# Where the square sums of each norm are made, and when attention bias and expert weights are asked for, in a hybrid SSD / RWKV-7 / attention / MoE trunk

## The reference

```
mod   = silu([c_ctx, c]) @ w_mod + b_mod               # 6 x 1024 values for context, 6 x 1024 for latent
h     = rmsnorm(x) * norm1 * (1 + mod[1]) + mod[0]     # adaLN, first norm
ssd   = rmsnorm(scan(h) * silu(z(h))) * ssd_norm       # branch A, with a norm of its own
rwkv  = ...                                            # branch B
att   = softmax(q k^T / 8 + na_bias + mask) v          # branch C, 2-D neighbourhood attention
x    += mod[2] * ((sum over branches of sigmoid(gate_b) * (branch_b @ w_branch_b)) @ w_out)
h     = rmsnorm(x) * norm2 * (1 + mod[4]) + mod[3]     # second norm
x    += mod[5] * moe(h)                                # 16 experts, two for each token
out   = rmsnorm(x_latent) * final_norm                 # after both layers
rmsnorm(x) = x / sqrt(mean(x * x) + 1e-6)
```

## Time and profile before

| what | us |
|---|---|
| median of 3 runs | 4776.42 |
| lowest and highest | 4769.83, 4780.67 |
| the profiled execution's own time | 4769.36 |
| its span, first to last instruction | 4767.6 |

### The profile page before, as it was taken

The page is one execution under the profiler, slowest core; times in us unless marked ns, Lnnn a source line. Parts: engine busy times, 40 slices in busy tenths (PEclk is TensorE's granted clock), DMA queues, the critical chain, the costliest instruction groups (busy, mean ns, idle before and its releaser), DMA issues. The chain is left out here.

```text
span 4767.6 us, 98189 instructions
## 1 busy us (share of the span) xinstructions
PE 4123.0 (86%) x42694; PEld 2762.9 (58%) x42694; DVE 1377.5 (29%) x2738; ACT 1029.6 (22%) x1751; POOL 452.8 (9%) x355
## 2 busy tenths in 40 slices
PE   6988997979999998969999488897798899986996
PEld 2453445437777785457887235655576777874332
DVE  1471003224554552110000045102154555512111
ACT  2211004213333331020000121103043333311101
POOL 0040003011111110000000002003011111100000
PEclk8999998989999998979999788998899999988998
DMA  7201221121000001168997710222211000035996
GB/s 281 71 1 53 71 71 49 40 91 31 18 20 18 18 3 54 53 215 299 319 314 261 274 52 33 88 88 71 59 32 31 18 20 18 3 107 226 396 403 254
DMA packets 299378, 539.47 MB, mean 113 GB/s; under 512 B 52272, under 2 KB 160064, under 8 KB 298832
## 3 DMA queue, kind: packets, MB, share of 16 engines
q1 hardware_dynamic: 291344, 505.80, 30.5%
q0 software_dynamic: 7616, 27.27, 1.6%
HBM read 515.13 MB, written 17.87 MB: 112 GB/s over the span
## 5 line engine op out<-in xcount | busy, mean ns | idle before, releaser
L1435 PE MATMUL bank<-inv 64*64 64x64 f32 x15104 | 491.5, 219 | 21.3 <-ACT inv L1723 9.7
L1435 PEld LDWEIGHTS bank<-inv 64*64 64x64 f32 x15104 | 468.3, 135 | 61.4 <-issue 59.9
L2578 PEld LDWEIGHTS bank<-xs,gu 128*128 128x128 f32 x3072 | 347.6, 193 | 8.5 <-issue 7.4
L255 PE MATMUL bank<-sb_h,ring 128*128 128x512 f32 (+1 forms) x768 | 315.9, 573 | 41.2 <-SPq L219 31.6
L2578 PE MATMUL bank<-xs,gu 128*128 128x96 f32 x3072 | 347.6, 276 | 1.0 <-DVE hid L2507 1.0
L1445 PE MATMUL bank<-sb_h,w 128*128 128x512 f32 (+1 forms) x768 | 319.0, 572 | 27.8 <-DMA w<-w_in 26.0
L255 PEld LDWEIGHTS bank<-sb_h,ring 128*128 128x128 f32 x768 | 149.9, 197 | 206.4 <-issue 192.5
L1445 PEld LDWEIGHTS bank<-sb_h,w 128*128 128x128 f32 x768 | 149.8, 197 | 182.9 <-issue 149.2
L490 PE MATMUL bank<-sb_h,ring 128*128 128x512 f32 (+1 forms) x512 | 179.4, 505 | 28.4 <-ACTq L502 23.0
L444 PE MATMUL bank<-sb_h,ring 128*128 128x512 f32 (+1 forms) x512 | 196.1, 544 | 5.5 <-SPq L219 3.7
L1185 DVE CUSTOM_DVE_ANT_0 sc<-bank,nabias 128x512 f32<-128x512 f32 (+1 forms) x96 | 53.8, 600 | 447.0 <-POOL nabias L1095 350.7
(11 more groups left out here) (362 smaller groups left out, 6222.0 us busy)
## 6 DMA issues: line engine op xcount, KB each, us to landing
mod_ring<-w_mod SPq DMA_DIRECT2D x24, 2048.0 KB, 23.0
ring<-w_in SPq DMA_DIRECT2D x24, 2048.0 KB, 7.9
gu<-moe_w_gate SPq DMA_DIRECT2D x128, 384.0 KB, 8.4
gu<-moe_w_up SPq DMA_DIRECT2D x128, 384.0 KB, 9.8
down<-moe_w_down SPq DMA_DIRECT2D x96, 512.0 KB, 4.5
gu<-moe_w_gate SPq DMA_DIRECT2D x64, 768.0 KB, 14.4
gu<-moe_w_up SPq DMA_DIRECT2D x64, 768.0 KB, 15.0
down<-moe_w_down SPq DMA_DIRECT2D x48, 1024.0 KB, 16.9
```

The source lines that it names most:

```text
L255: mm = nc.tensor.matmul(banks[j % len(banks)], ring[:, h, kt, P * j:P * j + P], rhs[:, kt], start=kt == 0, stop=kt == KT - 1)
L1435: m = mm(bank[hs, at:at + w], left(hs), right(hs), start=start, stop=True, skip_group_check=True)
L2578: m = mm(wide[j // 4][:, C * (j % 4):C * (j % 4) + C], w[:, P * j:P * j + P], xs[:, kt], start=kt == 0 and j % 4 == 0, stop=kt == KT - 1, ...
```

## The change

1. `modulation` takes in the first norm. In layer 1 it also does the residual of the experts, which had been a stage. `x` of layer 0 is asked for behind the fifth slab. Squares are added up by VectorE into one tile `k.ssq` of 128 by 512, and one matmul with ones (behind slab 9) sums it over the partitions.
2. `gate_by_z` and `residual_out` make the square sums for the norm behind them in the same way. What is left of those norms is `norm_branch` and `norm_tokens`.
3. The inverse root is Ln and Exp on ScalarE instead of a scale, Sqrt and reciprocal.
4. `norm_tokens` takes in the clearing, now on POOL.
5. `residual_out` asks for router, gate and up weights at its start (behind its own slabs), `norm_tokens` for the down weights.
6. `project_tokens` clears, fetches and masks the bias of the first two head pairs; `attend` does so for the other six.
7. `finish` is the end of the program in one stage: last residual, norm, and output in four pieces.

The core of the diff:

```diff
+def inverse_root(k, act, rinv, sums, done):
+    k.nc.scalar.activation(rinv, sums, ACT.Ln, scale=1.0 / D, bias=const(k, "eps")).then_inc(done, 1)
+    act.wait_ge(done, 1)
+    k.nc.scalar.activation(rinv, rinv, ACT.Exp, scale=-0.5).then_inc(done, 1)
...
 def modulation(k):
...
                 sp.dma_start(ring[:, n % NR], wv[:, 4 * hf:4 * hf + 4, 1024 * cb:1024 * cb + 1024]).then_inc(slabs[n % NR], 16)
+                if n == NR - 1 and l == 0:
+                    sp.dma_start(k.x[:], k.d.xT.rearrange("(kt p) t -> p kt t", p=P)).then_inc(s.tokens, 16)
...
+                if j == 3:
+                    squares(act)
+                if j == 9:
+                    act.wait_ge(s.mean, 1)
+                    inverse_root(k, act, rinv[:], sums, s.normed)
+            act.wait_ge(s.vec, 6)
+            for m in range(0, KT, 2):
+                for c in range(2):
+                    x = k.h[:, m, LC * c:LC * c + LC]
+                    nc.scalar.activation(x, x, ACT.Identity, bias=k.mod[:, m, c:c + 1], scale=k.nscale[:, 0, m, c:c + 1]).then_inc(s.affine, 1)
...
+                if n == 9:
+                    pe.wait_ge(s.summed, KT - 1)
+                    nc.tensor.matmul(sums, const(k, "ones"), k.ssq[:], start=True, stop=True).then_inc(s.mean, 1)
...
+            if l:
+                for m in range(KT):
+                    for c in range(2):
+                        x = k.x[:, m, LC * c:LC * c + LC]
+                        ins = nc.vector.scalar_tensor_tensor(x, k.acc[:, m, LC * c:LC * c + LC], k.mod[:, 40 + m, c:c + 1], x, ALU.mult, ALU.add)
+                    ins.then_inc(s.updated, 1)
+            for m in range(1, KT):
+                v.wait_ge(s.square, m + 1)
...
+                nc.vector.tensor_tensor(k.ssq[:], k.ssq[:], sq[:, m % 2], ALU.add).then_inc(s.summed, 1)
+            v.wait_ge(s.normed, 2)
+            for m in range(KT):
+                nc.vector.tensor_tensor(k.h[:, m], k.x[:, m], rinv[:], ALU.mult).then_inc(s.normed, 1)
...
+            for m in range(1, KT, 2):
+                for c in range(2):
+                    x = k.h[:, m, LC * c:LC * c + LC]
+                    nc.vector.tensor_scalar(x, x, k.nscale[:, 0, m, c:c + 1], k.mod[:, m, c:c + 1], ALU.mult, ALU.add).then_inc(s.affine, 1)
...
 def residual_out(k, t0):
...
             load_slabs(k, sp, s, k.d.w_out[l], 0, 1)
+            k.stream.begin(sp)
...
-def project_tokens(k, dst):
+def project_tokens(k, dst, bias):
...
+        @block.gpsimd
+        def _(pool):
+            nc.gpsimd.memset(bias[:], 0.0).then_inc(s.cleared, 1)
+            pool.wait_ge(s.bias, 2 * 8 * 16)
...
         @block.sync
         def _(sp):
+            sp.wait_ge(s.cleared, 1)
+            for f in range(2):
+                for to, src in bias_rows(k, bias, f):
+                    sp.dma_start(to, src).then_inc(s.bias, 16)
             take_first_slabs(k, sp, (s.loaded0, s.loaded1), 16)
             ask_next_slabs(k, sp, [(s.done, 4), (s.done, 8)])
...
 class WeightStream:
...
-        for g in range(KT):
-            if g < self.n_gu:
-                self.ask_gu(sp, g)
+        for g in range(self.n_gu):
+            self.ask_gu(sp, g)
+
+    def begin_down(self, sp):
         for d in range(self.n_down):
             self.ask_down(sp, d)
-        for g in range(KT, self.n_gu):
-            self.ask_gu(sp, g)
```

More of the change, by code:

```diff
@@ L364, in norm, with _ @@
     with ExitStack() as st:
[L365 to L369, removed]
-        block = st.enter_context(nc.Block())
[L372 to L375, removed]
+        s = st.enter_context(phase(nc, "sum root scaled moved cleared"))
+        rinv = st.enter_context(nc.sbuf_tensor(f"rinv_second{l}", [P, TT], F32))
+        block = st.enter_context(nc.Block())
+        @block.sync
+        def _(sp):
+            k.stream.begin_down(sp)
+        @block.tensor
+        def _(pe):
+            nc.tensor.matmul(k.bank[0][:, 0:n], const(k, "ones"), k.ssq[:, t0:], start=True, stop=True).then_inc(s.sum, 1)
[4 more added lines that the diff above has]
+            pool.wait_ge(s.cleared, len(cleared))
+        @block.vector
+        def _(v):
+            v.wait_ge(s.root, 2)
+            for m in range(KT):
+                nc.vector.tensor_tensor(k.h[:, m, t0:], k.x[:, m, t0:], rinv[:, t0:], ALU.mult).then_inc(s.scaled, 1)
         @block.scalar
         def _(act):
[L379 to L387, removed]
+            act.wait_ge(s.sum, 1)
+            inverse_root(k, act, rinv[:, t0:], k.bank[0][:, 0:n], s.root)
             for m in range(KT):
@@ L395, in _, with norm_branch @@
+def norm_branch(k, y, t0):
+    nc, l = k.nc, k.layer
+    n = TT - t0
+    with ExitStack() as st:
+        s = st.enter_context(phase(nc, "sum root scaled"))
+        rinv = st.enter_context(nc.sbuf_tensor(f"rinv_branch{l}", [P, TT], F32))
+        block = st.enter_context(nc.Block())
         @block.tensor
         def _(pe):
[L397 to L400, removed]
+            nc.tensor.matmul(k.bank[0][:, 0:n], const(k, "ones"), k.ssq[:, t0:], start=True, stop=True).then_inc(s.sum, 1)
+        @block.scalar
+        def _(act):
+            act.wait_ge(s.sum, 1)
+            inverse_root(k, act, rinv[:, t0:], k.bank[0][:, 0:n], s.root)
@@ L2714, in residual_ffn, with _ @@
         block = st.enter_context(nc.Block())
+        out = k.d.out.rearrange("(kt p) t -> p kt t", p=P)
+        @block.sync
+        def _(sp):
+            for m in range(0, KT, 2):
+                sp.wait_ge(s.scaled, m + 2)
+                sp.dma_start(out[:, m:m + 2], k.h[:, m:m + 2, LC:]).then_inc(s.stored, 16)
+            sp.wait_ge(s.stored, 16 * (KT // 2))
+        @block.scalar
+        def _(act):
+            for m in range(KT):
+                act.wait_ge(s.updated, m + 1)
+                if m >= 3:
+                    act.wait_ge(s.summed, m - 2)
+                nc.scalar.activation(sq[:, m % 2] if m else k.ssq[:, LC:], k.x[:, m, LC:], ACT.Square).then_inc(s.square, 1)
+            act.wait_ge(s.mean, 1)
+            inverse_root(k, act, rinv[:], k.bank[0][:, 0:LC], s.root)
@@ L2716, in _ @@
+        @block.tensor
+        def _(pe):
+            pe.wait_ge(s.summed, KT - 1)
+            nc.tensor.matmul(k.bank[0][:, 0:LC], const(k, "ones"), k.ssq[:, LC:], start=True, stop=True).then_inc(s.mean, 1)
         @block.vector
         def _(v):
-            for m in range(KT):
-                for c in range(t0 // LC, 2):
-                    x = k.x[:, m, LC * c:LC * c + LC]
-                    nc.vector.scalar_tensor_tensor(x, k.acc[:, m, LC * c:LC * c + LC], k.mod[:, 40 + m, c:c + 1], x, ALU.mult, ALU.add).then_inc(s.added, 1)
@@ new lines, in _ @@
+            for m in range(KT):
+                nc.vector.scalar_tensor_tensor(k.x[:, m, LC:], k.acc[:, m, LC:], k.mod[:, 40 + m, 1:2], k.x[:, m, LC:], ALU.mult, ALU.add).then_inc(s.updated, 1)
+                if m >= 3:
+                    add_square(m - 2)
+            add_square(KT - 2)
+            add_square(KT - 1)
+            v.wait_ge(s.root, 2)
+            for m in range(KT):
+                nc.vector.scalar_tensor_tensor(k.h[:, m, LC:], k.x[:, m, LC:], k.final[:, m:m + 1], rinv[:], ALU.mult, ALU.mult).then_inc(s.scaled, 1)
@@ L2808, in program @@
             experts_dense(k, flag, t0)
[L2809 to L2816 removed]
+        finish(k)
         for sem in (k.dt_in, *k.pool_dma):
```

217 lines of the change are left out of this document (127 added, 90 removed).

## The result

| | us |
|---|---|
| before, median of 4 runs | 4776.28 (4769.83 to 4780.67) |
| after, median of 4 runs | 4650.93 (4646.02 to 4656.87) |
| ratio | 0.9739, 95% interval 0.9722 to 0.9756 |
| forecast | 4681 (4664 to 4702) |

The change is faster, by 125 us and not by the 93 us of the forecast; the range misses it by 13 us. The profiled execution has a span of 4649.1 us, 118.5 us less than before. First the seams of the changed kernel, each cut as in the earlier trace rows (length, busy time of PE, PEld, DVE, ACT and POOL, granted clock, DMA share, GB/s): first norm of layers 0 and 1, branch norm of both, second norm of both, start of the value projection of both, end of the program. The last two lines are the attention stages.

The account below looks back on a forecast made before the run. The prediction took dense stages as bound by TensorE's matmuls, with time to win only at the seams. Its terms summed to 92.9 us (1.9%), giving a forecast of 4681 us, range 4664 to 4702.

Parts of the forecast that it names:

- the first one: Opening step: dense stages are bound by matmuls, the change touches only the seams between stages, so only those were priced.
- the forecast's own terms: Gains predicted for norms, FFN residual, attention bias and end, less 1 us for semaphores: 92.9 us in sum.
- the other stages lost 7 where I had 1: Semaphore term: some 16 more names cleared by SP between stages, 1 us lost (0 to 2).
- First norm: Start of each layer: norm work hidden beside modulation's weight slabs, gaining 15.8 us in layer 0 and 21.4 in layer 1.
- 5.2 for x: Layer 0 modulation: asking for x earlier makes later slabs and the stage's end 5.2 us later.
- 1.0 for the product: Layer 0 modulation: 1.0 us allowed for the product x*rinv not quite being done at the stage's end.
- Branch norms, second norm, end: Shorter chains at these seams: gains of 7.8 and 3.8 us, 10.2 and 19.4 us, and 6.8 us.
- the rival of one load for both: Ln and Exp share one table, saving a load at five seams: 6.4 us more, 4675 us; chance 10%.
- Attention bias: Bias moved into the value projection: the wait moves behind SP's issue there; 1.5 us gained for the whole part.
- "better" side of the second rival: Attention runs at granted clock 1.00 from its start, winning 5 and 2.5 us: 4674 us; chance 12%.
- the other side, a slow projection: Value projection starts at clock 0.50 and attention does not win it back, -7 us: 4690 us; chance 12%.
- "slower": Denser TensorE work makes the chip grant clock 0.50 inside dense stages: 4808 us; chance 3%.

Follow-up runs that it names:

- the fastest version: Changed kernel with TensorE's looped RWKV turns written out and landed value-projection slabs handed over before the bias transfers: 4563.84 us, ratio to before 0.9559.

## Why the prediction was wrong

**The step that failed** is the first one, "the change touches the seams between stages": only stages with an edit got a term. A change of the number of instructions on an engine is an edit to every loop behind it on that engine. The term that was missing is 28 us (9.4 + 18.7); with it the sum is 121 us and the time within 0.1% of what was measured, partly by luck, since the forecast's own terms come 3 us higher in the table and the other stages lost 7 where I had 1. The loss could be read before the change: 9.51 us of idle time "on issue" at the same instruction of each turn in layer 1, against 4.24 in layer 0, for the same code. I had put down the RWKV stages as dense and looked no further. Layer 1's head stood at the worst place of a block, so that nearly any other count of instructions ahead of it would win there; layer 0's could have gone either way, from 101 us a turn to 99 or to 103. Which of these the change brings needs a count of TensorE's instructions ahead of the loops in both programs, modulo 256.

**First norm.** Squares, sum and root lie beside the slabs, as forecast. Layer 0's modulation got longer by 7.5 us (last vector at 83.78, not 76.32), where I had 5.2 for x and 1.0 for the product; what stays outside is 7.25 us, of which the affine step is 4.04. Gain 13.3 instead of 15.8. This shortfall is no firm finding: from one trace to the next the same modulation stage of layer 0 took 77.7 to 81.7 us in the five runs with the old code of that stage and 87.6 to 89.9 in the nine with the new. Their means, 79.3 and 88.7, differ by 9.4 us and not by the 11.7 of the two traces compared here, and would give the gain as 15.6.

**Branch norms, second norm, end.** 13.5 against 12.9 us, 10.0 against 10.1, 16.0 against 16.0, 10.0 against 11.2, 25.6 against 25.9. Two table loads stand in every chain, seven for Ln and seven for Exp; the rival of one load for both does not hold here:

```profile
L186 ACT ACT_TABLE_LOAD x7 | 9.0, 1283 | 8.3 <-PEq L171 8.3
L188 ACT ACT_TABLE_LOAD x7 | 9.0, 1283 | 0.1
```

**Attention bias.** Right that the wait only moved: TensorE idles 15.78 us before L1160 in layer 0, where I had 14.6, and 15.99 in layer 1, where I had 15.3:

```profile
663.62 16.96 PE L1160 MATMUL bank<-ring,sb_h 128*128 128x512 f32 x34 [15.78 <-SPq L227]
3132.90 17.53 PE L1160 MATMUL bank<-ring,sb_h 128*128 128x512 f32 x37 [15.99 <-SPq L227]
```

Attention gained 23.1 and 16.7 us, not 15.3 and 16.0: its granted clock in layer 0 is 1.00 where it was 0.89. So by the two traces the "better" side of the second rival held in layer 0 (5 us there, of which the run with the bias moved back confirms about half), and the other side, a slow projection, cost little (0.87 in its first 16 us, 1.00 then). The real miss of this part was not to see that SP's order made the whole stall avoidable.

**Against "slower".** The granted clock did not fall with a denser TensorE: the mean over the span is 0.928 before and 0.937 after, 0.940 with turns written out and 0.942 in the fastest version. Fewer gaps gave clock back.

**Open.** The other stages lost 7 us where I had 1. The greatest part is 5 us in layer 1's scan, which took 105.9 us here and in one other run and 101 to 104 in the rest, most of them with the same change, so it is not the change's. The expert stages are 0.8 and 1.6 us longer and layer 0's router stage 0.9, all within what they vary by from run to run. (Layer 0's gate stage is 1.7 us longer for the squares; in the table that is inside the 7.4 us of the branch norm.) The turns of layer 1 gain another 1 us when a whole block is left: the stall of 1.1 to 1.4 us at 69 us into the turn is absent in both runs that have it so. Which of the later block boundaries stall and which don't was not worked out.

## What to carry to other kernels

Before pricing an edit, look for idle time "on issue" at the first instruction of a loop: here it was a jump waiting for code, 4 us each and up to 9.6, with some us at the low clock besides, and any edit ahead of the loop on that engine can move it either way. Write such turns out, or place the head so that over half a block follows it. When a wait is moved to another stage, list what stands behind it in the issuing queue there, and hand over first what has already landed.

## What the runs showed of the hardware

A jump back of TensorE to code that is not held cost 3.9 to 4.7 us. With about 4 instructions left in the target's block it cost 9.3 to 9.7 us; with 7 left a second stall of 2.3 to 3.4 us followed, with 45 to 59 left one of 0.9 to 3.5 us, with 119 or more none behind the head. Straight code showed no such gap at the head of a turn (0.77 us at the turns written out, ended by ScalarE), but stalls of 1.0 to 2.1 us inside seven of twelve turns. The granted clock was 0.50 for 3.4 to 10.2 us around each jump of the two kernels, and 1.00 through eleven of the twelve turns without one. At a granted clock of 0.50 a float32 matmul of 128x2 with its loads took 0.42 us.
